# A 32-byte table moves from ahead of the working area to behind it, so that the area starts 32 bytes lower

## The chip, the core and the metric

The kernel runs on one core of one Trainium2 chip. The metric is the device time of one execution in microseconds (us). Three executions of the kernel before took 1931.01, 1932.65 and 1935.12 us; the median, 1932.65 us, is the time to beat.

Five engines take part: TensorE (PE, matrix multiply, with its weight loads listed apart as PEld), VectorE (DVE), ScalarE (ACT), GpSimd (POOL) and SyncE (SP), which starts most transfers. The fast memory next to the engines, SBUF, has 128 partitions; every tensor here lies at one byte address that is the same in all partitions. The change is about those addresses.

## The reference, cut to what matters

Two two-layer blocks work one after the other on 256 tokens of width 1024, all in float32. The first has a Mamba-2 mixer in its first layer and block attention in its second, each between two gated feed-forwards; the second has a convolution module and a sparse attention, each followed by a feed-forward. In order: `ffn0`, `ssm`, `ffn1`, `ffn2`, `moba`, `ffn3`, `conf`, `cffn0`, `nsa`, `cffn1`. The six feed-forwards carry most of the arithmetic:

```python
D_MODEL, SEQ, D_FF = 1024, 256, 2816

def modulate(x, g, c_act, w, b):
    m = c_act @ w + b
    shift, scale, gate = jnp.split(m, 3, axis=-1)
    h = rmsnorm(x, g) * (1.0 + scale[:, None, :]) + shift[:, None, :]
    return h, gate[:, None, :]

def swiglu(h, w_gate, w_up, w_down):            # ffn0 to ffn3
    return (jax.nn.silu(h @ w_gate) * (h @ w_up)) @ w_down
...
        h, g = modulate(x, norm_g[i, 0], c_act, mod_w[i, 0], mod_b[i, 0])
        x = x + 0.5 * g * swiglu(h, ffn_w_gate[i, 0], ffn_w_up[i, 0], ffn_w_down[i, 0])
...
def conv_ffn(h, w_up, w_dw, b_dw, w_down):      # cffn0, cffn1
    a, v = jnp.split(h @ w_up, 2, axis=-1)
    return (jax.nn.silu(causal_dwconv(a, w_dw, b_dw)) * v) @ w_down
```

## The kernel before

**High and low parts.** Most of the large products are computed in the `float32r` format, in three passes. A weight tile of 128 x 2048 words comes by DMA into a slot of `ring`; ACT rounds it into `w_hi` (`high`, L1303) and DVE subtracts to get the rest, `w_lo` (`low`, L1633). The activations are split in the same way. PE then multiplies high by high, high weight by low activation, and low weight by high activation, and adds all three in PSUM. In each of these products one operand is loaded into the array (the weights, 128 columns, PEld) and the other streams past it (the activations, 256 or 258 columns, PE).

**Which pair of tables holds the activations.** Each stage has its own pair of high and low parts:

- the first half of each feed-forward (gate and up, L664) streams `Hs_hi` and `Hs_lo`, the scaled residual. A row of these tables has 258 words: 256 tokens, and two columns for the shift. `ffn0` to `ffn3` stream all 258, `cffn0` and `cffn1` 256. Row k starts 1032 bytes behind row k-1. The first three tiles of the convolution module stream the same tables, 256 columns, in the other order (L671 to L673);
- the second half (down, L671 to L673) streams `hid_hi` and `hid_lo`, rows of 256 words;
- the projections of `ssm` stream `H_hi_ssm` and `H_lo`, those of `moba` `H_hi_moba` and `H_lo` (L964; its last four tiles load these and stream the weights), the output projections `Z_hi` and `Z_lo`, `O_hi` and `O_lo`, the second product of the convolution module `CV_hi` and `CV_lo`. All of these have rows of 256 words.

**Two orders of the three passes.** `three` (L671, L672, L673) streams high, low, high for one result tile and then goes to the next. `woven` (L664) does two result tiles at once: high, high, low, low, high, high, for each of eight rows k.

**Where the tables lie.** `sb(...)` takes the next free bytes, in steps of 32. `h_at` is the start of `H`, and `Hs_lo` and `H_lo` are put there (they share the place with `H`). All the other tables of the list lie in `arena`, 24000 words, at fixed offsets from its start `arena_at`. Between `H` and `arena` lie `rstd`, `rtok`, `modv`, `modsc`, `gate`, `modraw` and `cact`. So the distance between a table in `arena` and one at `h_at` depends on how many bytes are between them. Two tables in `arena`, such as `hid_hi` and `hid_lo`, have a distance that their offsets alone give (the 160 words in the second are there to set it):

```python
hid_hi = rounded("hid_hi", 2 * L, 4, L)
hid_lo = rounded("hid_lo", 6 * L + 160, 4, L)
Hs_hi = rounded("Hs_hi", 32 * L, KD, LS)
Hs_lo = nc.alloc_sbuf_tensor_at("Hs_lo", [P, KD, LS], F32R, offset=h_at)
```

**What sets the order of the work.** Everything is written out by hand: one program per engine, with semaphores between them (`block.tensor`, `block.scalar`, `block.vector`, `block.gpsimd`, `block.sync`). A feed-forward is a loop in which PE does two gate-and-up tiles (96 matmuls at L664) and one down tile (48 at L671 to L673), again and again, while ACT and DVE split the next weight tiles and apply the activation, POOL scales, and SP refills the ring.

Of the kernel before, what the change touches and what calls it, by code (L numbers as in the profile page):

```python
# [29 lines left out]
P = 128  # L30
L = 256
D = 1024
KD = D // P
# [115 lines left out]
def build(nc, x_in, c_in, vec_in, small_in, con_in, mod_in, w_in, out):  # L149
    with ExitStack() as ctx:  # L150
        def sb(name, shape, dt=F32):
            return ctx.enter_context(nc.sbuf_tensor(name, shape, dt))
# [16 lines left out]
        rstd = sb("rstd", [P, 2 * L])  # L169
        rtok = sb("rtok", [P, 2])  # L170
        modv = sb("modv", [P, 24])
        modsc = sb("modsc", [P, KD])
        gate = sb("gate", [P, 2, KD])
        modraw = sb("modraw", [P, 2, 24])
        cact = sb("cact", [P, D])
        ARENA = 24000
        arena_at = nc.sbuf_base
        arena = sb("arena", [P, ARENA])

        def part(at, *shape):  # L180

            n = int(np.prod(shape))
            assert at + n <= ARENA
            v = arena[:, at:at + n]
            if len(shape) == 2:
                return v.rearrange("p (a b) -> p a b", a=shape[0])
            if len(shape) == 3:
                return v.rearrange("p (a b c) -> p a b c", a=shape[0], b=shape[1])
            return v
# [2249 lines left out]
```

## Time and profile before

| | |
|---|---|
| median of three executions | 1932.65 us |
| profiled execution, its own time | 1934.32 us |
| span of the profiled execution | 1932.2 us |
| mean granted TensorE clock | 0.97 of full speed |
| PE busy, PEld busy | 1831.6 us (95%), 1759.5 us (91%) |
| DVE, ACT, POOL busy | 1298.2, 924.7, 387.3 us |
| matmuls | 14410, of them 6336 at L664 |
| read from HBM | 368.89 MB, 191 GB/s over the span |

The profile names an instruction by its engine, its line in the kernel, and `out<-in`, the tables it writes and reads. A matmul's length in the trace (some 280 ns) is longer than the time from its start to the start of the next (some 118 ns), since several are in flight; the second of these, here called the pitch, sets how long a row of matmuls takes. It is read from start times, or from the view of the chain of waits, which merges neighbouring pieces of one line into one row with start, length and count.

### The profile page before, as it was taken

The numbers are of one execution on the slowest core, as the hardware profiler recorded it, in microseconds if no ns is written. First come the engines' busy times: TensorE is split into PE (matmuls) and PEld (weight loads), VectorE is DVE, ScalarE is ACT, GpSimd is POOL, SyncE is SP. The second block draws the span as 40 slices with busy tenths as digits, with TensorE's granted clock in tenths as the row PEclk, the third lists the DMA queues.
The fourth block names the chain that finished last, engine by engine and source line by source line (L and its number), as shares of the span: only waits on it lengthen the run. The fifth ranks groups of instructions, "written<-read, shape, count | busy, mean of one in ns | idle before, by whom it ended". The sixth has DMA issues, their size and how long they took to land.

```text
span 1932.2 us, 35876 instructions
## 1 busy us (share of the span) xinstructions
PE 1831.6 (95%) x14410; PEld 1759.5 (91%) x14410; DVE 1298.2 (67%) x1803; ACT 924.7 (48%) x1323; POOL 387.3 (20%) x381
## 2 busy tenths in 40 slices
PE   3999999999999999999899999979999999799998
PEld 2999999969999999999789999869999888479998
DVE  6676867887677667758855555986666333666665
ACT  3544555464544554454564446035544311575443
POOL 1222200071222222210233220003222000342221
PEclk9999899999999999999899999979999899699999
DMA  9877634826667657767535454404545334025552
GB/s 378 314 262 301 263 131 175 300 92 243 216 259 283 236 196 258 284 236 278 187 116 190 176 191 160 148 1 153 192 178 191 115 130 153 1 71 180 185 182 79
DMA packets 51058, 371.08 MB, mean 192 GB/s; under 512 B 5664, under 2 KB 5664, under 8 KB 6048
## 3 DMA queue, kind: packets, MB, share of 16 engines
q1 hardware_dynamic: 41760, 302.85, 43.3%
q0 software_dynamic: 9216, 67.11, 8.8%
q8 instruction: 55, 0.90, 0.2%
q14 instruction: 27, 0.22, 0.0%
HBM read 368.89 MB, written 1.05 MB: 191 GB/s over the span
## 4 chain that ended last, share of the span: by engine, by line
PE 80%; DVE 10%; ACT 4%; POOL 3%; issue 2%; DMA 1%; POOLq 0%; SPq 0%; DVEq 0%; ACTq 0%
PE gu L664 37%; PE acc L672 7%; PE acc L671 7%; PE acc L673 7%; PE gu L964 4%; DVE arena L2122 3%; PE gu L655 3%; PE gu L671 2%; PE gu L673 2%; PE gu L672 2%; DVE w_lo L1633 2%; DMA mring<-in_mods 1%; DVE arena L1914 1%; ACT Hs_hi L1286 1%; PE acc L1075 1%
## 5 line engine op out<-in xcount | busy, mean ns | idle before, releaser
L1633 DVE TENSOR_TENSOR w_lo<-ring,w_hi 128x2048 fp32r<-128x2048 f32 x255 | 595.1, 2336 | 261.5 <-ACT w_hi L1303 261.3
L1303 ACT ACTIVATE w_hi<-ring 128x2048 fp32r<-128x2048 f32 x255 | 486.3, 1908 | 105.2 <-PE acc L673 53.2
L664 PE MATMUL gu<-Hs_hi,w_hi 128*128 128x258 f32 (+1 forms) x2112 | 427.9, 284 | 2.9 <-DVE w_lo L1633 1.9
L664 PE MATMUL gu<-Hs_lo,w_hi 128*128 128x258 f32 (+1 forms) x2112 | 423.8, 282 | 0.0
L664 PE MATMUL gu<-Hs_hi,w_lo 128*128 128x258 f32 (+1 forms) x2112 | 423.1, 282 | 0.0
L584 POOL TENSOR_TENSOR arena<-arena,rstd 128x512 f32<-128x512 f32 x132 | 197.5, 1496 | 819.7 <-ACT arena L1317 783.4
L664 PEld LDWEIGHTS gu<-Hs_hi,w_hi 128*128 128x128 f32 x2112 | 326.5, 190 | 4.6 <-DVE w_lo L1633 2.0
L664 PEld LDWEIGHTS gu<-Hs_hi,w_lo 128*128 128x128 f32 x2112 | 326.5, 189 | 0.0
L664 PEld LDWEIGHTS gu<-Hs_lo,w_hi 128*128 128x128 f32 x2112 | 326.1, 190 | 0.0
L672 PE MATMUL acc<-hid_lo,w_hi 128*128 128x256 f32 x1056 | 297.8, 282 | 0.0
L671 PE MATMUL acc<-hid_hi,w_hi 128*128 128x256 f32 x1056 | 296.4, 281 | 0.8 <-DVE hid_lo L1846 0.8
L673 PE MATMUL acc<-hid_hi,w_lo 128*128 128x256 f32 x1056 | 295.9, 280 | 0.0
L671 PEld LDWEIGHTS acc<-hid_hi,w_hi 128*128 128x128 f32 x1056 | 198.9, 188 | 1.1 <-issue 1.1
L673 PEld LDWEIGHTS acc<-hid_hi,w_lo 128*128 128x128 f32 x1056 | 199.4, 189 | 0.0
L672 PEld LDWEIGHTS acc<-hid_lo,w_hi 128*128 128x128 f32 x1056 | 198.5, 188 | 0.0
L1338 ACT ACTIVATE hid_hi<-arena 128x256 fp32r<-128x256 f32 x132 | 55.2, 418 | 291.4 <-DVE arena L1837 200.7
L1648 DVE SCALAR_TENSOR_TENSOR mring<-mring,cact 128x1024 f32<-128x1024 f32 x144 | 170.2, 1221 | 11.0 <-DMA mring<-in_mods 10.8
L1317 ACT ACTIVATE arena<-gu 128x516 f32<-128x516 f32 (+1 forms) x132 | 78.4, 594 | 143.0 <-PE gu L664 139.7
L671 PE MATMUL gu<-H_hi_ssm,w_hi 128*128 128x256 f32 x384 | 111.0, 289 | 4.4 <-DVE w_lo L1633 2.5
L673 PE MATMUL gu<-H_hi_ssm,w_lo 128*128 128x256 f32 x384 | 109.4, 285 | 0.0
L672 PE MATMUL gu<-H_lo,w_hi 128*128 128x256 f32 x384 | 109.2, 284 | 0.0
L1846 DVE TENSOR_TENSOR hid_lo<-arena,hid_hi 128x256 fp32r<-128x256 f32 x132 | 70.0, 530 | 57.6 <-ACT hid_hi L1338 57.6
(348 smaller groups left out, 2782.5 us busy)
## 6 DMA issues: line engine op xcount, KB each, us to landing
ring<-in_weights SPq DMA_DIRECT2D x276, 1024.0 KB, 4.8
mring<-in_mods POOLq DMA_DIRECT2D x64, 1024.0 KB, 6.1
mring<-in_mods SPq DMA_DIRECT2D x8, 1024.0 KB, 7.5
con<-in_constants SPq DMA_DIRECT2D x1, 1408.0 KB, 11.9
X<-in_x SPq DMA_DIRECT2D x1, 1024.0 KB, 7.0
out<-X SPq DMA_DIRECT2D x1, 1024.0 KB, 3.9
cact<-in_c SPq DMA_DIRECT2D x1, 512.0 KB, 3.3
vec<-in_vectors SPq DMA_DIRECT2D x1, 498.0 KB, 4.1
```

The source lines that it names most:

```text
L584: pool.tensor_tensor(both, both, row.unsqueeze(1).to_broadcast([P, 2, L]), ALU.mult).then_inc(scaled_ready, 1)
L655: ins = mm(bank[:, e * L:(e + 1) * L], w[:, k * L + e * P:k * L + (e + 1) * P], src[:, k, :], start=(k == 0 and e == 0), stop=(k == KD - 1 ...
L664: ins = mm(dst, part, x_lo if i == 1 else x_hi, start=start and i == 0, stop=stop and i == 2, skip_group_check=True)
L671: mm(dst, hi, x_hi, start=start, stop=False, skip_group_check=True)
L672: mm(dst, hi, x_lo, start=False, stop=False, skip_group_check=True)
L673: return mm(dst, lo, x_hi, start=False, stop=stop, skip_group_check=True)
L964: ins = mm(bank[:, e * L:(e + 1) * L], a, b, start=(k == 0 and e == 0 and i == 0), stop=(k == KD - 1 and i == 2), skip_group_check=True)
L1303: act.activation(w_hi[buffer_of(n0, s)][:, :], ring[:, n % RING, :], ACT.Copy).then_inc(hi_ready, 1)
L1317: act.activation(c[:, :, 0:width], gu[:, 2 * (f % 2):2 * (f % 2) + 2, 0:width], ACT.Copy).then_inc(pair_free, 1)
L1633: dve.tensor_tensor(w_lo[b][:, :], ring[:, n % RING, :], w_hi[b][:, :].bitcast(F32), ALU.subtract).then_inc(split_ready, 1)
L1648: ins = dve.scalar_tensor_tensor(out=w, in0=w, scalar=1.0, in1=cact[:, :], op0=ALU.mult, op1=ALU.mult, accum_out=total)
L1846: dve.tensor_tensor(hid_lo[:, f % 4, :], o, hid_hi[:, f % 4, :].bitcast(F32), ALU.subtract).then_inc(hid_ready, 1)
```

## The change

The allocation of `modsc`, eight words per partition (32 bytes), moves from between `modv` and `gate` to behind `arena`. `modsc` holds the eight scales of the current modulation; DVE writes it and ACT and DVE read it as a per-partition scalar.

```diff
         modv = sb("modv", [P, 24])
-        modsc = sb("modsc", [P, KD])
         gate = sb("gate", [P, 2, KD])
         modraw = sb("modraw", [P, 2, 24])
         cact = sb("cact", [P, D])
         ARENA = 24000
         arena_at = nc.sbuf_base
         arena = sb("arena", [P, ARENA])
+        modsc = sb("modsc", [P, KD])
```

So `gate`, `modraw`, `cact` and all that lies in `arena` start 32 bytes lower, and nothing else but `modsc` moves. The byte addresses modulo 1024, from the allocations of the two programs:

| table | before | after |
|---|---|---|
| `ring`, `mring`, `vec` | 128 | 128 |
| `X`, `H`, `Hs_lo`, `H_lo` | 320 | 320 |
| `w_hi`, `w_lo` (all three buffers) | 480 | 448 |
| `Hs_hi`, `H_hi_moba` | 736 | 704 |
| `H_hi_ssm` | 480 | 448 |
| `hid_hi`, `CV_hi` | 736 | 704 |
| `hid_lo`, `CV_lo` | 352 | 320 |
| `O_hi`, `O_lo`, `Z_hi`, `Z_lo` | 736 | 704 |

From a high part to its low part it is, modulo 1024:

| pair | before | after |
|---|---|---|
| `Hs_hi` to `Hs_lo` | 608 | 640 |
| `H_hi_moba` to `H_lo` | 608 | 640 |
| `H_hi_ssm` to `H_lo` | 864 | 896 |
| `hid_hi` to `hid_lo`, `CV_hi` to `CV_lo` | 640 | 640 |
| `O_hi` to `O_lo`, `Z_hi` to `Z_lo` | 0 | 0 |

The instructions and their order are the same on all five engines; only addresses in them differ. From the weights to `Hs_lo` and `H_lo` it was 864 bytes modulo 1024 and is 896; from the weights to every table in `arena` the distance stays.

## Rows read from the trace of the kernel before

**Rows 1.** The page, busy time: engine, us (share of the span) xinstructions
```profile
PE 1831.6 (95%) x14410; PEld 1759.5 (91%) x14410; DVE 1298.2 (67%) x1803; ACT 924.7 (48%) x1323; POOL 387.3 (20%) x381
```
**Rows 2.** The page, chain that ended last, by engine and by line
```profile
PE 80%; DVE 10%; ACT 4%; POOL 3%; issue 2%; DMA 1%; POOLq 0%; SPq 0%; DVEq 0%; ACTq 0%
...
PE gu L664 37%; PE acc L672 7%; PE acc L671 7%; PE acc L673 7%; PE gu L964 4%; DVE arena L2122 3%; PE gu L655 3%; PE gu L671 2%; PE gu L673 2%; PE gu L672 2%; DVE w_lo L1633 2%; DMA mring<-in_mods 1%; DVE arena L1914 1%; ACT Hs_hi L1286 1%; PE acc L1075 1%
```
**Rows 3.** Chain of waits, 512.8 to 530.3 us (ffn1): start us, us, what
```profile
512.84 11.43 PE gu L664 x96
524.28 0.12 PE acc L671
...
529.58 0.12 PE acc L671
...
529.94 0.36 PE gu L664 x3
```
**Rows 4.** Chain of waits, 1357 to 1392 us (cffn0)
```profile
1357.21 11.40 PE gu L664 x96
1368.61 0.12 PE acc L671
...
1374.27 11.40 PE gu L664 x96
```
**Rows 5.** Busy time in one turn of each loop: stretch, length, engines, PEclk, DMA, GB/s
```profile
core 0: us, PE busy (x) PEld busy (x) DVE busy (x) ACT busy (x) POOL busy (x), PEclk, DMA share, GB/s
512.84:529.94 17.10, 17.10 (x147) 17.10 (x146) 10.92 (x13) 8.66 (x10) 3.84 (x4) 1.00 0.78 279
1357.21:1374.27 17.06, 17.06 (x146) 17.06 (x146) 10.99 (x13) 8.46 (x10) 4.41 (x3) 1.00 0.52 185
```
**Rows 6.** Groups by line and shape: xcount | busy us, mean ns
```profile
L664 PE MATMUL gu<-Hs_hi,w_hi 128*128 128x258 f32 x1408 | 286.6, 285 | 2.6 <-DVE w_lo L1633 1.5 <-DVE Hs_lo L1696 1.0
L664 PE MATMUL gu<-Hs_hi,w_hi 128*128 128x256 f32 x704 | 141.3, 282 | 0.3 <-DVE w_lo L1633 0.3
```
**Rows 7.** Chain of waits, moba's projections: activations streamed, then weights streamed
```profile
885.62 34.04 PE gu L964 x289
919.54 22.85 PE gu L964 x192
```
**Rows 8.** Matmuls in order of time, ssm's last projections, 239 starts apart
```profile
361.38 0.28 PE L671 MATMUL gu<-H_hi_ssm,w_hi 128*128 128x256 f32 x1
...
389.53 0.28 PE L673 MATMUL gu<-H_hi_ssm,w_lo 128*128 128x256 f32 x1
```
**Rows 9.** The same, convolution module, second product, 46 starts apart
```profile
1320.12 0.28 PE L671 MATMUL acc<-CV_hi,w_hi 128*128 128x256 f32 x1
...
1325.54 0.28 PE L672 MATMUL acc<-CV_lo,w_hi 128*128 128x256 f32 x1
```
**Rows 10.** The same, moba's output projection, 142 starts apart
```profile
981.18 0.28 PE L671 MATMUL acc<-O_hi,w_hi 128*128 128x256 f32 x1
...
998.23 0.28 PE L672 MATMUL acc<-O_lo,w_hi 128*128 128x256 f32 x1
```
**Rows 11.** The same, convolution module, first product, 45 starts apart
```profile
1189.22 0.28 PE L671 MATMUL gu<-Hs_hi,w_hi 128*128 128x256 f32 x1
...
1194.59 0.28 PE L671 MATMUL gu<-Hs_hi,w_hi 128*128 128x256 f32 x1
```
**Rows 12.** Groups by line, DVE, 265 to 345 us (ssm) and 1210 to 1290 us (conf)
```profile
L1914 DVE SCALAR_TENSOR_TENSOR arena<-gu,vec,arena 128x255 f32<-128x255 f32 (+2 forms) x78 | 31.6, 475 | 23.2 <-ACT arena L1366 23.2
L1633 DVE TENSOR_TENSOR w_lo<-ring,w_hi 128x2048 fp32r<-128x2048 f32 x13 | 29.7, 2284 | 0.0
...
L2122 DVE SCALAR_TENSOR_TENSOR arena<-arena,vec 128x256 f32<-128x256 f32 x161 | 65.4, 484 | 0.0
```
**Rows 13.** Line L2122: duration ns min/median/max, first and last start us
```profile
L2122 DVE SCALAR_TENSOR_TENSOR arena<-arena,vec x166: 479/484/491, 1207.0 to 1284.5; 128x256 f32<-128x256 f32 x166
```

## The prediction

> **What bounds the kernel now.** I read the busy time first: PE is busy for 1831.6 of 1932.2 us, DVE for 67% and ACT for 48% [rows 1]. A matmul's length overlaps that of the next, so this alone doesn't say that PE is the bound; the chain that ended last does: 80% of it is PE, 37% the gate-and-up products at L664 and 21% the down products at L671 to L673 [rows 2]. The next view was the same chain within a loop. One turn of ffn1's loop, from 512.84 to 529.94 us, is 96 matmuls at L664 in one piece and then 48 down matmuls, with no other engine between them; cffn0's turn is the same [rows 3, 4]. In those turns DVE is busy for 10.92 of 17.10 us and ACT for 8.66, the DMA engines at 0.78 or 0.52, and the granted clock is 1.00, the 2.4 GHz level [rows 5]. So there the time is the number of matmuls times the pitch, and nothing is hidden on PE: a nanosecond in the pitch at L664 comes through in full. What else is late has room: DVE and ACT could do the turn in two thirds of it.
>
> **What the pitch depends on.** All pitches below are start to start, at the granted clock 1.00. 256 columns at 2.4 GHz are 106.7 ns, and 258 are 107.5.
>
> - L664 with 258 columns: 11.43 us / 96 = 119.1 ns [rows 3].
> - L664 with 256 columns: 11.40 / 96 = 118.7 ns [rows 4].
> - down, hid tables, distance 640: from 524.28 to 529.94 us 48 matmuls, 5.66 / 48 = 117.9 ns [rows 3, 5].
> - moba with the activations streamed, distance 608: 34.04 / 289 = 117.8 ns [rows 7]. ssm, distance 864: (389.53 - 361.38) / 239 = 117.8 ns [rows 8]. Convolution module's second product, distance 640: 5.42 / 46 = 117.8 ns [rows 9].
> - output projection, distance 0: 17.05 / 142 = 120.1 ns [rows 10].
> - first product of the convolution module, distance 608, but rows 1032 bytes apart: 5.37 / 45 = 119.3 ns [rows 11].
> - moba with the weights streamed and the activations loaded: 22.85 / 192 = 119.0 ns [rows 7].
>
> These have one shape, one clock and no wait in them, and they differ by 2.3 ns, so addresses do matter to PE here. The 0 case is the dearest; 608, 640 and 864 cost the same to 0.1 ns where rows are 1024 bytes apart.
>
> The Trainium skill says otherwise. In "TensorE: Matmul & The Clock Gate", section "Step-by-step: what each phase is for", the streamed operand and the weight load have a read port each, and a load takes nothing from the running matmul; "SBUF — State Buffer", section "Who interferes with whom", says that PE and ACT never wait on anyone. By these rules no address could alter a pitch and the change would do nothing at all. This trace does not agree with the general form: 120.1 against 117.8 ns for products that differ in where their tables lie [rows 8, 10].
>
> **The change part by part.** It removes and adds no instruction and no wait. What could cost or save is in four parts, against the profiled execution's own 1934.32 us (span 1932.2), which is 1.67 us over the median of the three.
>
> 1. L664, 1408 x 3 = 4224 matmuls with 258 columns and 704 x 3 = 2112 with 256 [rows 6], and 144 of the convolution module's first product in the other order. Their distance goes from 608 to 640. The nearest pair of rows to tell what that is worth is moba (608, high part at 736, low part at 320, weights at 480) and hid or CV (640, 736, 352, 480): 117.8 and 117.8 to 117.9 ns, no difference. And the nearest row to tell why Hs is 1.3 to 1.5 ns dearer is moba against the first product of the convolution module: the same order of passes, the same start addresses of all tables modulo 1024, the same distance; only the row step is 1032 in place of 1024 bytes, and the pitch is 119.3 in place of 117.8 [rows 7, 11]. What makes Hs dear is thus the row step, which the change leaves alone. I take 0 for this part. Bounds: at best all Hs products come down to 117.8 (118.6 for 258 columns, 0.8 ns being two more columns): 4224 x 0.52 = 2.2 us, 2112 x 0.95 = 2.0 us and 144 x 1.5 = 0.2 us, together 4.4 us saved. At worst they go up to the distance-0 level, 120.0 (120.8 for 258): 4224 x 1.7 = 7.2, 2112 x 1.3 = 2.7, 144 x 0.7 = 0.1, together 10.0 us lost.
> 2. H_lo with H_hi_ssm (864 to 896) and H_hi_moba (608 to 640). In ssm the first 16 tiles wait for DVE, so only the last eight count, 384 matmuls; in moba eight tiles with the activations streamed, 384, and four with the weights streamed, 192. By the equal rows for 608, 640 and 864 this is 0. Bounds: 960 x 2.2 = 2.1 us lost if they fall to the distance-0 pitch; 192 x 1.2 = 0.2 us saved if the last four tiles reach 117.8.
> 3. Products whose tables all lie in arena (down, O, Z, CV). Every distance among them and to the weights stays; only the common start moves by 32 bytes. H_hi_ssm at 480 and H_hi_moba at 736 gave one pitch [rows 7, 8], so I take 0. They are 3168 down matmuls; I give them no bound of their own but widen the range for it.
> 4. DVE and ACT instructions that read ring or vec (at 128) and arena, now 32 bytes further apart. DVE is the bound in two places: ssm's first tiles, where 78 taps take 31.6 us and 13 weight splits 29.7, and the convolution, 161 taps of 484 ns [rows 12]. The taps read rows of UP at any of 31 word offsets, and all 166 take 479 to 491 ns [rows 13], so an offset moves them by 7 ns at most and on average by nothing. 0. Behind that cover lies up to 166 x 7 ns = 1.2 us either way. modsc is read as one word per partition; its place costs nothing that a row shows.
>
> The sum is 0: 1934.3 us for an execution like the profiled one, and against the median 1932.65. I put the forecast at 1932.5.
>
> **The rivals.**
>
> *The distance is what matters, and 640 is better for woven rows too.* For it speaks that distance 0 costs 2.2 ns more than 640, so distance has an effect, and that in the woven order a low row follows a high row only once in six matmuls each way, not as in the equal pairs above, which are all of the other order. Against it: 608 and 640 are alike in three rows. It gives between 2 and 4.4 us less; at the full 4.4, 1928.2 us. It could go below that if the woven order has a floor under 117.8, of which the trace has no row.
>
> *640 is a whole multiple of 128 bytes, as 0 is, and 608 is not; with rows that start at 8, 16, ... 56 bytes past a 64-byte mark the high and the low row now stand at the same place in it.* This is the case that ends on the other side. Its place is L664. It speaks for it that O and Z, where both parts stand at the same place, show the dearest pitch; against it that hid, also a multiple of 128 apart, shows 117.9. If Hs goes all the way to the 120.0 level the loss is 10.0 us, 1942.6 us; if halfway, 5 us, 1937.6. It decides from 0.6 ns more per L664 matmul (6336 x 0.6 = 3.8 us).
>
> *The edit does nothing to PE at all,* which is also what the two rules named above amount to: the same number as the forecast, 1932.65, with every pitch unchanged to 0.1 ns. I count it into the forecast's case, since the time can't tell them apart, but the trace will.
>
> **How the numbers follow.** A change of 0.2%, 3.9 us, is about what a measurement of this kernel can tell from none; the three runs lie 4.1 us apart. No change within that: 0.52, which takes in the untouched pitch and small shifts of up to 0.6 ns at L664. The first rival in full or beyond: 0.27. The second: 0.21. The range: down to 1928.0, the full saving of 4.4 us; up to 1938.0, a little over half of the way to the distance-0 pitch. The forecast's own range is 1930 to 1935.
>
> **What would show it right or wrong.** In the changed kernel's chain of waits, a turn of ffn1's loop: 11.43 us for 96 matmuls again, and 17.10 for the turn. 11.38 or less would be the first rival, 11.50 or more the second. In the convolution module's first product 119.3 ns should stand; if it falls to 117.8 the row step was not the cause. moba's and ssm's projections should stay at 117.8, the down products at 117.9, the output projections at 120.0. If the down products move, the start address as such counts, and part 3 was wrong. If all pitches stay and the time still moves, it is in DVE: the taps at 484 ns and the splits at 2284 ns are where to look. What would make the prediction wrong is a dependence of the woven order on the distance that the rows of the other order don't show.

## The result, and the profile after

The changed kernel takes 1940.07 us, the median of six executions (1938.67 to 1942.11). The kernel before took 1932.09 us in the same comparison (six executions, 1930.52 to 1935.12). The ratio is 1.0040 [1.0027, 1.0052]: slower by 0.4%. The forecast was no change, 1932.5 us, with 1938.0 as the upper end of its range.

The busy time of the profiled execution of the kernel after (span 1937.7 us, its own time 1939.77 us, mean granted clock 0.970), engine, us (share of the span) xinstructions:

```profile
PE 1836.9 (95%) x14404; PEld 1765.0 (91%) x14410; DVE 1298.7 (67%) x1803; ACT 925.5 (48%) x1323; POOL 387.3 (20%) x381
```

Against [rows 1] PE has 5.3 us more, in a span that is 5.5 us longer; DVE has 0.5, ACT 0.8, POOL nothing. The next view is the chain of waits through ffn1, where [rows 3] showed 11.43 us for 96 matmuls and 17.10 us for a turn (columns: start us, us, what):

```profile
511.44 11.55 PE gu L664 x96
522.98 0.12 PE acc L671
...
528.64 11.54 PE gu L664 x96
...
545.85 11.54 PE gu L664 x96
```

and in cffn0, where [rows 4] showed 11.40 and 17.06:

```profile
1362.14 11.39 PE gu L664 x96
...
1379.18 11.39 PE gu L664 x96
```

The first product of ffn1 went from 11.43 / 96 = 119.1 to 11.545 / 96 = 120.25 ns per matmul, and the turn from 17.10 to 17.20 us. In cffn0, whose rows are streamed with 256 columns and not 258, it fell by 0.01 us per 96, some 0.1 ns. The down products between 522.98 and 528.64 us take 528.64 - 522.98 = 5.66 us for 48, the 117.9 ns of before. Both turns are still PE without a gap, with DVE and ACT far from full (the columns are those of [rows 5]):

```profile
511.44:528.64 17.20, 17.20 (x146) 17.20 (x146) 10.87 (x13) 8.67 (x10) 3.76 (x4) 1.00 0.74 263
1362.14:1379.18 17.04, 17.04 (x146) 17.04 (x146) 10.98 (x13) 8.45 (x10) 4.38 (x3) 1.00 0.52 186
```

The clock in them is at the 2.4 GHz level, as before. The other pairs stayed. Here the output projection, 142 starts apart (matmuls in order of time, as [rows 10]):

```profile
979.24 0.28 PE L672 MATMUL acc<-O_lo,w_hi 128*128 128x256 f32 x1
...
996.27 0.28 PE L673 MATMUL acc<-O_hi,w_lo 128*128 128x256 f32 x1
```

17.03 / 142 = 119.9 ns. The projections of moba and ssm gave 117.8, moba's last four tiles 119.0 and the first tile of the convolution module's first product 119.2, each within 0.1 ns of before. The down products of cffn0 and cffn1 went from 117.9 to 117.7, and the last 77 matmuls of that first product from 119.1 to 118.8; both together are worth under 0.2 us.

So one group of matmuls got longer. Its worth is 4224 x 1.12 ns = 4.7 us, less 2112 x 0.11 = 0.2 us: 4.5 us, 0.23%. It builds up by 0.11 us in each of the 40 turns of ffn0 to ffn3. That is less than the 8 us of the first comparison; the part on the size of the loss comes back to it.

### The profile page after: what moved, and what is told of

It is laid out like the page before. It is cut to its first block, busy times and chain, and to the rows that moved or that the text cites. A ratio compares the mean times of both kernels' runs of the same rounds, so it can differ in the third digit from the quotient of the medians.

```text
span 1937.7 us, 35870 instructions
## 1 busy us (share of the span) xinstructions
PE 1836.9 (95%) x14404; PEld 1765.0 (91%) x14410; DVE 1298.7 (67%) x1803; ACT 925.5 (48%) x1323; POOL 387.3 (20%) x381
## 4 chain that ended last, share of the span: by engine, by line
PE 80%; DVE 10%; ACT 4%; POOL 3%; issue 2%; DMA 1%; POOLq 0%; SPq 0%; DVEq 0%; ACTq 0%
PE gu L664 37%; PE acc L672 7%; PE acc L671 7%; PE acc L673 7%; PE gu L964 4%; DVE arena L2122 3%; PE gu L655 3%; PE gu L671 2%; PE gu L672 2%; PE gu L673 2%; DVE w_lo L1633 2%; DMA mring<-in_mods 1%; DVE arena L1914 1%; PE acc L1075 1%; ACT Hs_hi L1286 1%
## 5 line engine op out<-in xcount | busy, mean ns | idle before, releaser
L664 PE MATMUL gu<-Hs_hi,w_hi 128*128 128x258 f32 (+1 forms) x2112 | 425.4, 283 | 3.5 <-DVE w_lo L1633 1.9
L664 PE MATMUL gu<-Hs_lo,w_hi 128*128 128x258 f32 (+1 forms) x2112 | 425.9, 283 | 0.0
L664 PE MATMUL gu<-Hs_hi,w_lo 128*128 128x258 f32 (+1 forms) x2112 | 425.3, 283 | 0.0
L664 PEld LDWEIGHTS gu<-Hs_hi,w_hi 128*128 128x128 f32 x2112 | 326.4, 189 | 5.4 <-DVE w_lo L1633 2.0
L664 PEld LDWEIGHTS gu<-Hs_hi,w_lo 128*128 128x128 f32 x2112 | 327.6, 190 | 0.0
L664 PEld LDWEIGHTS gu<-Hs_lo,w_hi 128*128 128x128 f32 x2112 | 325.7, 189 | 0.0
```

The lines of the kernel that those rows point to most:

```text
L664: ins = mm(dst, part, x_lo if i == 1 else x_hi, start=start and i == 0, stop=stop and i == 2, skip_group_check=True)
```

## The experiments

Distances are from here on modulo 256 bytes where nothing else is said, since `sweep_d` shows that 256 is the period: `v` is the distance from the weights to the high part, `d` from the high to the low part. Before: Hs has v = 0, d = 96 (that is 608). After: v = 0, d = 128 (640).

### Which table's place counts?

Theory: the distance from `Hs_hi` to `Hs_lo`. Rival: the start address of `arena` and all that lies in it. Both differ between the two kernels; these two programs separate them.

`h_up` is the kernel before with `modsc` ahead of `H`, so that `arena` stays where it was and `H`, `Hs_lo` and `H_lo` go up by 32 bytes:

```diff
+        modsc = sb("modsc", [P, KD])
         H = sb("H", [P, KD, L])
...
-        modsc = sb("modsc", [P, KD])
```

> The 32-byte table modsc stands ahead of H in place of behind modv: H, Hs_lo and H_lo start 32 bytes higher (352 modulo 1024), the arena stays at 736 and the weights at 480 as in the kernel before. So high to low is 640, as in the changed kernel, but no table of the arena has moved. If only the relative places count (theory), a piece of 96 matmuls with 258 columns at L664 takes 11.54 us as in the changed kernel, and that with 256 columns 11.39. If the arena's own start counts (rival), it takes 11.43 us as in the kernel before.

`all_down` is the kernel before with the table `eps` behind `arena`, so that everything from `X` on starts 32 bytes lower and all distances stay:

```diff
-        eps = sb("eps", [P, 1])
...
         arena = sb("arena", [P, ARENA])
+        eps = sb("eps", [P, 1])
```

> eps, 32 bytes, moves from ahead of X and H to behind the arena: H and arena both start 32 bytes lower than before, high to low stays 608, the arena is where the changed kernel has it (704, weights 448), H is at 288. If only relative places count: 11.43 us for 96 matmuls with 258 columns, the kernel's time as before. If the arena's own start counts: 11.54 us.

The chain in ffn1, of `h_up` and then of `all_down`:

```profile
511.22 11.54 PE gu L664 x96
528.43 11.54 PE gu L664 x96
```

```profile
512.51 11.43 PE gu L664 x96
529.60 11.43 PE gu L664 x96
```

With `arena` unmoved and the distance 640 the pitch is 120.2 ns; with `arena` lower and the distance 608 it is 119.1. The distance counts, and the rival falls. (The single times, 1934.86 and 1938.09 us, go the other way; the part on the size says why a single time tells nothing here.)

`w_up` is the kernel after with eight more words in `arena`, so that `w_hi` and `w_lo`, which come last in it, are back at 480. The pair of Hs keeps d = 128, but v becomes 224:

```diff
-        ARENA = 24000
+        ARENA = 24008
```

> The changed kernel with an arena of 24008 words, which puts the weights' tables 32 bytes higher, back at 480: high at 704, low at 320, distance 640, and from the weights to the low part 864 as in the kernel before (from the weights to the high part 224 where both have 256). If the distance from high to low decides: 11.54 us for 96 matmuls with 258 columns. If the distance from the weights to the low part decides: 11.43 us. A third value would say that all three places count together.

```profile
510.32 11.48 PE gu L664 x96
527.42 11.48 PE gu L664 x96
```

11.48 / 96 = 119.6 ns, between the other two, and here the products whose three tables all lie in `arena` changed too. The output projection, 142 starts apart:

```profile
976.99 0.28 PE L673 MATMUL acc<-O_hi,w_lo 128*128 128x256 f32 x1
...
993.80 0.28 PE L671 MATMUL acc<-O_hi,w_hi 128*128 128x256 f32 x1
```

16.81 / 142 = 118.4 ns where it was 120.1 [rows 10]; the down products fell from 117.9 to 117.1. So the place of the weights counts as well, and the pitch is a matter of three tables, not of two. In `h_up` the low part moved against the weights as well as against the high part; `w_up` has it back at the old distance from the weights, and the pitch is neither the old one nor the new.

### Is it PE alone?

`sweep_d` leaves the whole network out and writes `x` to the output. Its PE runs 96 products at a time (the expectations of this and the next sweep say 192; the traces have 96), in the orders of the kernel, on three tables whose places are set for each piece, while all other engines are idle; v = 0 throughout and d goes through 1024 bytes. (`w` is the woven order, `t` the down order; then row step, columns, and the places of weights, high and low part.)

```python
CASES += [("w", 258, 258, 480, 736, 736 + d) for d in range(0, 1024, 32)]
CASES += [("w", 258, 256, 480, 736, 736 + d) for d in range(0, 1024, 32)]
CASES += [("t", 256, 256, 480, 736, 736 + d) for d in range(0, 1024, 64)]
CASES += [("w", 258, 258, 480, 736, 736 + d) for d in (608, 640)] * 2
```

> Not the network: PE alone. Matmuls in float32r in the woven order over eight rows, weights at 480, high at 736, and the low part at every distance from 0 to 992 in steps of 32 bytes, 192 matmuls each, with 258 and with 256 columns and a row step of 1032 bytes; then the order of the down product with rows of 1024 bytes. All other engines are idle. If the pitch is a matter of PE's own reads, 608 gives 119.1 and 640 120.25 ns with 258 columns, 118.7 and 118.6 with 256; if it comes from other engines' accesses to the same memory, all distances give one pitch. If 640 is bad because it is a multiple of 128, then 0, 128, 256, 384, 512, 768 and 896 are as bad.

The chain of this program, d = 544, 576, 608, 640, 672, 704 in turn:

```profile
255.76 11.45 PE acc L206 x96
267.22 11.49 PE gu L199 x96
278.71 11.44 PE acc L206 x96
290.15 11.56 PE gu L199 x96
301.70 11.51 PE acc L206 x96
313.22 11.53 PE gu L199 x96
```

The third row is the distance of before, 11.44 / 96 = 119.2 ns, the fourth that of after, 120.4. With DVE, ACT, POOL and DMA idle, PE shows the step of the two kernels to 0.2 ns. No rival that puts the step down to another engine's accesses is left. These rows leave one other: the pieces write `gu` and `acc` by turns, so that 608 goes with `acc` and 640 with `gu`. The last four pieces, 608, 640, 608, 640, have it the other way round:

```profile
974.33 11.43 PE gu L199 x96
985.76 11.55 PE acc L206 x96
997.32 11.45 PE gu L199 x96
1008.76 11.55 PE acc L206 x96
```

The step stays with the distance, whichever table is written. Over the 1024 bytes the values repeated every 256, to 0.4 ns. `sweep_w` then varied both v and d, 8 x 8 places in steps of 32 bytes for each of three forms, and `sweep_step` varied d in steps of 8 bytes, the distance from row to row, and the order.

> PE alone again, 192 matmuls per place, now over both distances: from the weights to the high part (v, 0 to 224 in steps of 32 bytes) and from the high to the low part (d, 0 to 224), for the woven order with 258 and 256 columns at a row step of 1032 bytes and for the down order with rows of 1024 bytes. The last sweep repeated itself every 256 bytes, so this covers all. If only d counts, the eight rows of v are equal. The run with the weights 32 bytes higher says they are not: at v = 224 and d = 128 I expect 119.6 ns with 258 columns, 118.7 with 256, 117.1 in the down order, and 118.4 there at d = 0; at v = 0 the numbers of the last sweep. Somewhere in the table lies a place under 119.0 ns for 258 columns; if none does, the kernel before stands at the best place already.

> PE alone, weights 480 and high 736 as before. First the distance from high to low in steps of 8 bytes, woven, 258 columns, row step 1032. Then for distances 0 to 224 in steps of 32: the down order with 258 columns; woven with 258 columns at row steps of 1056, 1088 and 1280 bytes; woven with 256 columns at 1024; the down order with 256 columns at 1032. My prediction blamed the row step of 1032 bytes for the 1.3 ns that the residual's products cost over the aligned ones. If that is right, woven at 1280 with 258 columns falls to about 118.6 at the distances 96 and 128 alike, and woven with 256 columns at 1024 to 117.8. If it is the woven order itself, these stay at 119 and 118.7, and the down order at 1032 falls. If the steps of 8 bytes move the pitch as much as those of 32, the address counts finer than a 32-byte table can set it.

At the place of `w_up` (v = 224, d = 128) `sweep_w` gave 119.6 ns with 258 columns and 117.1 in the down order, and 118.3 there at d = 0, as the kernel itself.

Pitch in ns for v = 0, from the chain's pieces of 96 matmuls:

| form | d = 0 | 32 | 64 | 96 | 128 | 160 | 192 | 224 |
|---|---|---|---|---|---|---|---|---|
| woven, 258 columns, rows 1032 bytes apart | 120.0 | 119.2 | 119.7 | **119.2** | **120.4** | 119.9 | 120.1 | 119.0 |
| woven, 256 columns, rows 1032 apart | 118.8 | 118.7 | 118.7 | 118.6 | 119.0 | 119.2 | 118.6 | 118.8 |
| woven, 256, rows 1024 apart | 120.0 | 119.9 | 118.8 | 118.9 | 118.2 | 118.9 | 118.9 | 118.8 |
| woven, 258, rows 1280 apart | 120.8 | 119.5 | 120.0 | 120.1 | 122.2 | 121.0 | 121.1 | 120.1 |
| down order, 256, rows 1024 apart | 119.9 | 120.0 | 117.9 | 117.8 | 117.8 | 117.8 | 117.8 | 118.7 |
| down order, 256, rows 1032 apart | 118.9 | 118.2 | 118.7 | 119.1 | 118.8 | 119.3 | 118.5 | 118.5 |
| down order, 258, rows 1032 apart | 119.9 | 119.7 | 119.7 | 120.2 | 119.7 | 119.4 | 120.0 | 120.0 |

Woven with 258 columns was also run with rows 1056 and 1088 bytes apart: 119.6 to 121.0 ns. A place that came again among other neighbours differed by up to 0.4 ns, and at one place by more: the down order with rows of 1024 bytes at d = 128 was at 117.8 here and at 116.7 in all four pieces of `sweep_d`. So differences of that size within a row mean little.

Several things follow. The change moved the product from one of the three cheapest places of its row to the dearest. The down order with rows of 1024 bytes has a plateau of 117.8 from 64 to 192, and 96 (moba, ssm) and 128 (hid, CV) both lie on it, as 0 (O, Z) does not. In the down order the same two distances stand the other way round, 120.2 at 96 and 119.7 at 128 with 258 columns, so an order can't speak for another. Woven with 256 columns and rows of 1032 bytes the whole row is within 0.7 ns. And with rows 1280 bytes apart, 256 times five, the two places are 2.2 ns apart where it was 1.2, so it is not the 8 bytes over 1024 in the row step that make this product dear: I had expected 118.6 there. Steps of 8 bytes count as much as steps of 32: from d = 96 to 128 they give 119.1, 119.0, 119.4, 120.0 and 120.3, with no common rule such as a multiple of 64 or 128. Over the whole grid the first form went from 119.0 to 120.8 and the down order with 256 columns and rows of 1024 bytes from 113.3 (v = 64, d = 0) to 121.1 (v = 128, d = 64).

### A better place

The grid has a place for rows of 1024 bytes that is 4.5 ns below what the kernel shows. `w64` brings the tables of that step to v = 64, d = 0 by moving the weights up by 192 bytes and taking 128 bytes out of the offsets of `hid_lo` and `CV_lo`:

```diff
-        ARENA = 24000
+        ARENA = 24048
...
-        hid_lo = rounded("hid_lo", 6 * L + 160, 4, L)
+        hid_lo = rounded("hid_lo", 6 * L + 128, 4, L)
...
-        CV_lo = rounded("CV_lo", 5120 + L + 160, KD, L)
+        CV_lo = rounded("CV_lo", 5120 + L + 128, KD, L)
```

> The kernel before, with an arena of 24048 words, which puts the weights' tables 192 bytes higher, so that every high part in the arena lies 64 bytes (modulo 256) above them; hid_lo and CV_lo move by 32 words to a distance of 0 modulo 256 from their high parts, which O and Z have already. By the sweep of PE alone (113.3 ns at v = 64, d = 0 in the down order, 117.8 at v = 64, d = 96, 119.6 with 258 columns at v = 64, d = 96) the down products fall from 117.9 to 113.3 ns, 3168 x 4.6 = 14.6 us, O and Z from 120 to 113.3, and L664 with 258 columns rises by 0.45 ns, 4224 x 0.45 = 1.9 us: about 1920 us. If the sweep doesn't carry over to the kernel, because outputs, neighbours or the other engines matter, the pitches stay near 118 and the time near 1934.

```profile
508.46 11.50 PE gu L664 x96
525.61 11.50 PE gu L664 x96
```

The output projections came down to 117.8 ns, but the down products stayed at 117.8 too and were to reach 113.3; Hs, now at v = 64, d = 96, went to 11.50 / 96 = 119.8 (119.6 in the sweep), and with 256 columns in cffn0 from 118.7 to 119.5 (119.5 in the sweep). One time, 1936.89 us, where about 1920 was expected. A miss, and an odd one: the same place, a pitch 4.5 ns higher.

`aligned` goes further. It gives each form the best place of its row: Hs v = 0, d = 224; the tables with rows of 1024 bytes v = 64, d = 0; and the residual for cffn0, cffn1 and the convolution module gets tables of its own with rows of 256 words, in the down order. Of the edit, beside that of `w64`:

```diff
+        pad = sb("pad", [P, 24])
...
+        Hs_hi = rounded("Hs_hi", 32 * L + 48, KD, LS)
+        Hs_lo = nc.alloc_sbuf_tensor_at("Hs_lo", [P, KD, LS], F32R, offset=h_at + 160)
+        Cs_hi = rounded("Cs_hi", 32 * L, KD, L)
+        Cs_lo = nc.alloc_sbuf_tensor_at("Cs_lo", [P, KD, L], F32R, offset=h_at)
...
+                            for e in range(2):
+                                ins = three(gu[:, 2 * (f % 2) + e, 0:L], buffer_of(n0, s),
```

> The same, and beside it 96 bytes ahead of the arena, so that H_lo lies at a distance of 0 modulo 256 from H_hi_ssm and H_hi_moba; tables Cs with rows of 1024 bytes in place of Hs for cffn0, cffn1 and the convolution module, in the down order; and Hs for the other four feed-forwards at v = 0, d = 224, the best place of the sweep. By the sweep: the 256-column products of cffn0 and cffn1 fall from 118.7 to 113.3 ns, 2112 x 5.4 = 11.4 us, moba's and ssm's by 4.5 ns in some 800 matmuls, 3.5 us, down by 14.6, O and Z by 2 to 3, L664 with 258 columns stays at 119.1: about 1900 us. If the down order at L664 suffers from something the sweep has not (each result tile in its own bank), less.

```profile
522.05 11.41 PE gu L667 x96
533.47 0.11 PE acc L674
...
538.79 0.11 PE acc L676
538.91 6.19 PE gu L667 x52
```

Hs is at 11.41 / 96 = 118.9 ns, and the 48 down products between 533.47 and 538.91 us now take 5.44 us, 113.3 ns each. A turn takes 16.86 us instead of 17.10. In cffn0 and cffn1 the down products and the products of the new tables, which stand at the same v and d, were at 117.8, and so were the output projections. One time: 1919.35 us, where about 1900 was expected.

Why does one place give 113.3 in ffn0 to ffn3 and 117.8 in cffn0? `sweep_fine` ran that place again between others.

> PE alone. The down order with rows of 1024 bytes, high to low 0, 8 and 248, weights to high 0 to 120 in steps of 8: is 113.3 ns at v = 64, d = 0 a point or a valley? Then woven with 256 columns and rows of 1024 bytes over both distances; the down order with 258 columns at a row step of 1280, d = 0; and at the end v = 64, d = 0 again after different neighbours. If a pitch belongs to a place alone, every return to v = 64, d = 0 gives 113.3; the last two sweeps gave 116.7 and 117.8 for v = 0, d = 128, which came after different neighbours, so I expect that one to take two values.

Down order, 256 columns, rows of 1024 bytes; (v, d) is (64, 0), (0, 0), (64, 0), (0, 128), (64, 0), (0, 96), (0, 128), (0, 64), (0, 128) in turn:

```profile
1424.44 11.30 PE gu L213 x96
1435.74 11.51 PE acc L220 x96
1447.25 10.88 PE gu L213 x96
1458.13 11.30 PE acc L220 x96
1469.43 10.88 PE gu L213 x96
1480.32 11.31 PE acc L220 x96
1491.62 11.31 PE gu L213 x96
1502.93 11.32 PE acc L220 x96
1514.25 11.20 PE gu L213 x96
```

The same program on the same tables: (64, 0) takes 11.30 us the first time and 10.88 twice after; (0, 128) takes 11.30, 11.31 and then 11.20. A place has more than one pitch, 117.7 and 113.3, or 117.8 and 116.7, and a whole piece of 96 runs at one of them. Within this program what ran before is all that differs between the pieces, and for (0, 128) there is a pattern: the five pieces that followed (0, 64), here and in `sweep_d`, took 116.7, the three that followed (64, 0) or (0, 96), here and in `sweep_w`, 117.8. What of it selects the pitch was not found. Nor was the width of the low place: ahead of these pieces the same program had (64, 0) in this order once at 117.8, and no place 8 bytes from it in v or d came below 117.8. Two variants of `aligned` asked whether its edits in cffn0 and cffn1 matter. `aligned_woven` has the woven order there; `aligned_hs` leaves these stages on the tables of Hs with rows of 1032 bytes, in the woven order:

```diff
-        Cs_hi = rounded("Cs_hi", 32 * L, KD, L)
-        Cs_lo = nc.alloc_sbuf_tensor_at("Cs_lo", [P, KD, L], F32R, offset=h_at)
+        Cs_hi, Cs_lo = Hs_hi[:, :, 0:L], Hs_lo[:, :, 0:L]
```

> The version with all pairs at v = 64, d = 0, whose down products fell to 113.3 ns in ffn0 to ffn3 but stayed at 117.8 in cffn0 and cffn1, now with the woven order for cffn0 and cffn1 (rows of 1024 bytes). The sweep has 113.3 ns for that order too. If which of its two pitches a place takes hangs on how PE comes into it, the other order may let both products of cffn fall to 113.3 (9 us less than the 1919 of the down order) or leave them at 117.8.

> The same, with cffn0, cffn1 and the convolution module on the Hs tables at v = 0, d = 224 as the other feed-forwards, woven, 256 columns at a row step of 1032 bytes. The sweep has 118.8 ns for that, 1.0 more than the 117.8 of the last version, but coming from there the down products may fall to 113.3 as they do in ffn0 to ffn3: 2112 x 1.0 = +2.1 us against 1056 x 4.5 = -4.7 us.

The first product of cffn0 was at 117.8 ns in the woven order too, and at 118.9 on the tables of Hs (before: 118.7); the down products there were at 117.8 and 117.9, in ffn0 to ffn3 at 113.3 in both. One time each, 1924.02 and 1924.93 us. So neither the order nor the tables of the product ahead makes cffn's down products slow by itself. What else of the stage does was not separated.

What ran before isn't the whole answer either. `aligned` was profiled a second time (as `aligned_timed`, below), the same program with the same addresses. The second product of the convolution module, at (64, 0), in the first execution and then in the second, 95 starts apart:

```profile
1299.78 0.28 PE L675 MATMUL acc<-CV_lo,w_hi 128*128 128x256 f32 x1
...
1310.54 0.28 PE L674 MATMUL gu<-Cs_hi,w_hi 128*128 128x256 f32 x1
```

```profile
1304.94 0.28 PE L675 MATMUL acc<-CV_lo,w_hi 128*128 128x256 f32 x1
...
1316.13 0.28 PE L674 MATMUL gu<-Cs_hi,w_hi 128*128 128x256 f32 x1
```

10.76 / 95 = 113.3 ns and 11.19 / 95 = 117.8 ns. The list of instructions is the same, so something that differs from one execution to the next, their timing perhaps, takes part in the choice. In the loops the pitches did repeat: in all four executions of `aligned` and its two variants the down products took 113.3 ns in ffn0 to ffn3 and 117.8 or 117.9 in cffn0 and cffn1, but for the last tile of cffn1 in `aligned_woven`, 113.3.

### Necessary, and enough

Two programs with one number changed each, and eleven executions of each timed. `lo_back` is the kernel after, with `Hs_lo` alone moved so that d is 96 again (864 modulo 1024); `arena` stays in its new place:

```diff
-        Hs_lo = nc.alloc_sbuf_tensor_at("Hs_lo", [P, KD, LS], F32R, offset=h_at)
+        Hs_lo = nc.alloc_sbuf_tensor_at("Hs_lo", [P, KD, LS], F32R, offset=h_at + 224)
```

> The changed kernel with Hs_lo alone 224 bytes higher (544 modulo 1024), so that the residual's parts lie 864 bytes apart, 96 modulo 256 as the 608 of the kernel before; H_lo, hid, CV, O, Z and the weights stay where the changed kernel has them. If the loss is all in the residual's pair, 96 matmuls with 258 columns take 11.43 us again and the time is that of the kernel before within 2 us. If the arena's lower start costs something elsewhere (rival: the loops explain 4.4 to 4.7 of the 5.5 to 8 us), 11.43 us come back but 1 to 3 us of the time stay lost.

`lo_640` is the kernel before, with `Hs_lo` alone 32 bytes higher, so that the distance is 640 and nothing else has moved:

```diff
-        Hs_lo = nc.alloc_sbuf_tensor_at("Hs_lo", [P, KD, LS], F32R, offset=h_at)
+        Hs_lo = nc.alloc_sbuf_tensor_at("Hs_lo", [P, KD, LS], F32R, offset=h_at + 32)
```

> The kernel before with Hs_lo alone 32 bytes higher, so that the residual's parts lie 640 bytes apart and nothing else moves. If the residual's pair is the whole cause, a piece of 96 matmuls takes 11.54 us and the time is that of the changed kernel; if the changed kernel loses a part of it elsewhere, this one is faster than it by that part.

The chain in ffn1, of `lo_back` and then of `lo_640`:

```profile
512.98 11.43 PE gu L664 x96
530.07 11.43 PE gu L664 x96
```

```profile
510.94 11.54 PE gu L664 x96
528.14 11.54 PE gu L664 x96
```

`lo_back` stands to the kernel before at 0.9995 [0.9986, 1.0004]: the loss is gone. `lo_640` stands at 1.0028 [1.0018, 1.0038]: the loss is there with this one offset. The cause is settled on that level: the place of `Hs_lo` against `Hs_hi` and the weights, in products with 258 columns in the woven order.

The kernel after itself and `aligned` were timed again beside `lo_640`, on one chip:

> The changed kernel once more, beside the others on one chip. The loops' pitch explains 4224 x 1.12 = 4.7 us less 0.2 us, 4.5 us over the kernel before; the first timing gave 8.0 us, with an interval of 5.2 to 10.0 us. If the pitch is all, the ratio comes out near 1.0023; if something else in the change costs 3 us more, near 1.004.

> The version with every pair of 256-column tables at v = 64, d = 0 and the residual's at v = 0, d = 224, timed: 40 loop turns with 48 down matmuls at 113.3 in place of 118.0 ns (1920 with the loops' last ones, 2112 in all, 4.7 ns, 9.9 us), 2112 matmuls of cffn at 117.8 in place of 118.7 (2.0 us), 4224 at 118.9 in place of 119.1 (0.9 us), O and Z 2.2 ns in 640 matmuls (1.4 us): about 14 us less than the kernel before, a ratio of 0.9927.

| kernel | median us (lowest to highest) | ratio to before |
|---|---|---|
| before (21 executions) | 1934.63 (1931.53 to 1937.78) | |
| after (12) | 1936.51 (1932.85 to 1941.12) | 1.0010 [1.0001, 1.0020] |
| `lo_640` (11) | 1940.53 (1934.65 to 1942.18) | 1.0028 [1.0018, 1.0038] |
| `aligned` (6) | 1922.73 (1918.16 to 1927.34) | 0.9938 [0.9922, 0.9954] |

`aligned` beats both kernels, the kernel before by 12 us or 0.6%. 2112 down products x (118.0 - 113.3) ns = 9.9 us of this, 4224 at Hs x 0.2 = 0.8, 2112 in cffn0 and cffn1 x 0.95 = 2.0, and 768 in the output projections x 2.2 = 1.7: 14.4 us together. With the clock taken out, as in the next part, the executions give 13.8.

### The size of the loss

The kernel after and `lo_640` have one pitch in every loop and differ by 0.2% in these medians, and the two comparisons of the kernel after give 1.0040 and 1.0010, whose intervals don't meet. Executions of one kernel lie up to 9 us apart. The profiled executions tell what most of this is, the time for which the granted clock is at 1.2 GHz and not at 2.4. Added up within the span from the record of the clock in each trace, with half of it (what a stretch bound by PE loses) taken off the span:

| kernel | distance of Hs | span us | at 1.2 GHz us | span less half of it |
|---|---|---|---|---|
| before | 96 | 1932.2 | 114.0 | 1875.1 |
| `all_down` | 96 | 1936.2 | 124.0 | 1874.2 |
| `lo_back` | 96 | 1936.9 | 124.0 | 1874.9 |
| `h_up` | 128 | 1932.9 | 110.5 | 1877.7 |
| after | 128 | 1937.7 | 117.4 | 1879.0 |
| after, second time | 128 | 1934.2 | 110.6 | 1879.0 |
| `lo_640` | 128 | 1932.6 | 107.0 | 1879.1 |
| `aligned` | 224 | 1917.4 | 113.5 | 1860.6 |
| `aligned`, second time | 224 | 1922.3 | 120.1 | 1862.3 |

The spans of the first seven overlap. The last column has two groups, 1874.2 to 1875.1 and 1877.7 to 1879.1, 3.9 us apart by their means, against 4.5 us from the pitches. The clock moves a single execution by more than the change does, and that is why `lo_640` had the shorter span (1932.6) beside a slower kernel, and `all_down` the longer beside an equal one.

The same can be done with every timed execution, since each has its span and its mean granted clock (to 0.001) on record, and their product is the span less half of the time at 1.2 GHz. Means of these products:

| kernels | distance of Hs | executions | product us | mean clock |
|---|---|---|---|---|
| before | 96 | 36 | 1874.2 | 0.9698 |
| `lo_back` | 96 | 11 | 1874.4 | 0.9700 |
| after | 128 | 18 | 1878.6 | 0.9704 |
| `lo_640` | 128 | 11 | 1878.9 | 0.9699 |

All 47 executions at 96 lie from 1872.0 to 1876.8, all 29 at 128 from 1876.8 to 1881.3, and their means are 4.4 us apart. That is the loss, 0.23%, and it is what the pitches give. The first comparison's 8 us and the second's 2 us lie on both sides of it: the kernel after had a mean clock of 0.9695 in the first and 0.9709 in the second, which alone is some 2.8 us. The distance itself doesn't lengthen the time at the lower level: the mean clock is 0.9698 at 96 and 0.9702 at 128. Taking off half is rough, since it holds only where PE is the bound.

## Why the prediction was wrong

*What bounds the kernel* was right: PE without a gap in the loops, so a nanosecond at L664 came through in full, once for each of the 4224 products with 258 columns.

*Part 1 failed.* It put the term of L664 at 0, and the 4224 products with 258 columns took 1.12 ns more each, 4.7 us. It took the equal pitch of 608 and 640 in moba, hid and CV for a rule about distances, and carried it to L664. All of these stream 256 columns in the down order with rows of 1024 bytes. L664 is woven, with 258 columns. In its own form 96 and 128 are 119.2 and 120.4 ns, and in the down order with 258 columns their order is reversed. The three equal rows were three samples of one form, 117.8 each, and not evidence on another. The bounds of this part (4.4 us saved, 10.0 lost) did hold the loss of 4.5 us, and with 1932.1 + 4.5 = 1936.6 us so would the range. That the six executions came out at 1940.07 goes with their mean clock, 0.9695 against 0.9709 in the second comparison; the prediction had no term for that.

*The row step as the cause* was carried too far in the same way. The 1.5 ns between moba's row and the convolution module's [rows 7, 11] were taken for the price of rows 1032 bytes apart. In the form of these two rows, the down order with 256 columns, the sweeps bear that out: at d = 96 it is 117.8 ns with rows of 1024 bytes and 119.1 with 1032. For L664 they don't: woven with 256 columns at d = 96 it is 118.9 at 1024 and 118.6 at 1032, and with 258 columns and rows 1280 apart it went from 119.5 to 122.2 with the place. The row step has no price of its own that holds from form to form, and `lo_back` and `lo_640` give the Hs product 119.1 and 120.2 at one row step.

*The sentence on what would make the prediction wrong* named this case: a dependence of the woven order on the distance that the rows of the other order don't show.

*Part 2* held: moba and ssm stayed at 117.8, moba's last four tiles at 119.0. *Part 3* held within 0.2 ns for down, O, Z and CV, and `all_down` agrees: a common shift by 32 bytes doesn't count. *Part 4* held: DVE has 0.5 us more busy time in 1298.7, and `lo_back`, in which the taps read their rows 32 bytes lower as in the kernel after, is as fast as the kernel before.

*The rivals.* The first (640 better) fell: 258 columns got dearer, and 256 columns fell by 0.1 ns. The second came nearest: 11.55 us is past its mark of 11.50, and its case of half the loss was 1937.6 us where the pitches give 1936.6. But only the 258 columns got dearer, not all of Hs. Its reason was wrong: a multiple of 128 as such is nothing, for d = 160 and 192 cost as much as d = 0 in that row, and the down order's 640 isn't dear. The third, the edit that does nothing, fell. What `sweep_d` shows against it: only addresses differ between its rows, and they take 11.44 to 11.56 us.

The Trainium skill gives the streamed operand and the weight load a read port each ("TensorE: Matmul & The Clock Gate", section "Step-by-step: what each phase is for"); by that alone `sweep_d` would show one number, and it shows 119.0 to 120.4 ns. Whether the two reads get in each other's way or something else in PE depends on the places isn't shown. The same page's section "Back-to-back issue gap" gives N/2.4 + 2.5 ns for matmuls in isolation, by which 256 columns are an estimate of 109.2 ns, and says that in a stream with weight loads both operations set the gap; no product of 256 columns in these forms came to 109.2, the nearest to 113.3. That PE never waits on another engine, as the Trainium skill says ("SBUF — State Buffer", section "Who interferes with whom"), agrees with the trace for Hs: `sweep_d`, with the others idle, gives the pitches of the full kernel to 0.2 ns. For the place (64, 0), which has 113.3 or 117.8 ns in the kernel, it isn't shown.

*The chances.* 0.52 for no change rested on part 1. With no row of a woven product at another distance, the equal rows should have moved the chances less, towards the bounds.

## What to carry to other kernels

Where PE is the bound and loads weights for every matmul, the places of its three tables modulo 256 bytes are a parameter worth 1% to 4% of the pitch; they cost a few bytes of padding to change, and any edit that shifts one of them against another changes them unseen. A pitch read in one form (order of passes, columns, row step) says nothing of another form, so it is to be measured in the form in question, in the kernel itself, since a bare loop of PE gave 113.3 where the kernel gave 117.8. And for a change of 0.2% the pitch in the chain of waits is the measurement: it repeated to 0.01 us in 11.5, while times of one kernel scattered by 8 us. Where the granted clock of each execution is known, span times clock takes most of that scatter out.

## What the runs showed of the hardware

- The pitch of a float32r product of 128 x 128 by 256 columns at 2.4 GHz went from 113.3 to 121.1 ns with nothing but the places of the tables altered, and all other engines idle. With 258 columns and rows 1032 bytes apart it went from 119.0 to 120.8. The low part's place repeats every 256 bytes to 0.4 ns (`sweep_d`), and 8 bytes matter (119.4 to 120.0 ns).
- A common shift of all three tables by 32 bytes changed nothing (119.1 ns in `all_down`).
- One place can have two pitches, 113.3 and 117.7 ns, or 116.7 and 117.8, held for whole pieces of 96 matmuls. What ran before goes with it in the sweeps (`sweep_fine`), but two executions of one program also differed (`aligned`: 113.3 and 117.8 ns).
- What in PE's reads produces these numbers stays open: no simple rule of v and d was found in the 8 x 8 grid.
- The time at the lower clock level differed from one execution to the next by up to 17 us (107.0 to 124.0) for kernels with the same instructions, whatever the distance.
